# Rows of u broadcast by DMA instead of by TensorE in the mLSTM attention of a two-layer decoder trunk

## The reference, cut to what matters

```python
b = jnp.cumsum(lf, axis=-1)
logD = b[..., :, None] - b[..., None, :] + li[..., None, :]
m_t = jnp.maximum(inter, jnp.max(logD, axis=-1))
w_intra = jnp.exp(logD - m_t[..., None])           # exp(u[t] + w[s]), u = b - m_t, w = li - b
s = jnp.einsum('bhtd,bhsd->bhts', qc, kc) * w_intra
num = w_inter[..., None] * einsum(qc, C) + einsum(s, vc)
h = num / max(|den|, exp(-m_t))
C_new = decay[..., None, None] * C + jnp.einsum('bhs,bhsd,bhse->bhde', ws, kc, vc)
```

## Time and profile before

| | |
|---|---|
| median of 3 runs | 1389.44 us (1386.63 to 1391.36) |
| the profiled execution, its own time | 1389.6 us |
| its span | 1387.8 us, mean granted clock 0.98 |
| PE / PE weight load busy | 1334.1 us (96%) / 1289.9 us (93%) |
| DVE / ACT / POOL busy | 660.6 / 442.6 / 367.7 us (48%, 32%, 26%) |
| stage of the heads | about 211 us to 308 us of the span |

### The profile page before, as it was taken

How to read it: one execution, slowest core, us unless ns; L and a number is a source line. 1 busy time by engine, 2 the same in 40 slices (tenths; PEclk the granted TensorE clock), 3 DMA queues, 4 the chain that set the end, 5 groups by cost and what they waited for, 6 DMA issues and landing times.

```text
span 1387.8 us, 25466 instructions
## 1 busy us (share of the span) xinstructions
PE 1334.1 (96%) x10119; PEld 1289.9 (93%) x10119; DVE 660.6 (48%) x846; ACT 442.6 (32%) x672; POOL 367.7 (26%) x368
## 2 busy tenths in 40 slices
PE   4999999999999999999999896999999999999998
PEld 3999996779999999999999886999999999999997
DVE  6662333665794573343344693343533433333443
ACT  4311133432342241241341235322521422422423
POOL 3000004433799990000018561122000000000032
PEclk9999998999999999999999997999999999999999
DMA  5233231113332232223224985222222232323231
GB/s 146 62 84 84 76 91 28 53 43 76 92 88 79 78 89 80 87 76 90 76 76 141 155 138 130 85 81 85 77 83 84 76 90 76 91 76 91 76 89 72
DMA packets 239139, 119.55 MB, mean 86 GB/s; under 512 B 35512, under 2 KB 235888, under 8 KB 239088
## 3 DMA queue, kind: packets, MB, share of 16 engines
q1 hardware_dynamic: 238832, 118.78, 32.6%
q10 hardware_dynamic: 256, 0.06, 0.0%
HBM read 108.08 MB, written 10.73 MB: 86 GB/s over the span
## 4 chain that ended last, share of the span: by engine, by line
PE 85%; SPq 5%; DVE 5%; issue 1%; ACT 1%; DMA 1%; POOL 0%; DVEq 0%; ACTq 0%; POOLq 0%
PE ps L310 76%; SPq L521 2%; PE ps L1550 2%; PE ps L1577 2%; SPq L548 1%; DVE wlo L294 1%; DMA d_y<-U 1%; PE ps L1540 1%; PE ps L1586 1%; PE ps L1580 1%; DVE R L331 1%; PE ps L1603 1%; PE ps L1791 1%; SPq L502 0%; DVE xg_lo L360 0%
## 5 line engine op out<-in xcount | busy, mean ns | idle before, releaser
L289 ACT ACTIVATE whi<-raw 128x1024 fp32r<-128x1024 f32 x177 | 187.0, 1057 | 503.3 <-PE ps L310 491.0
L310 PE MATMUL ps<-hid_hi,whi 128*128 128x288 f32 x1408 | 302.9, 296 | 11.5 <-DVE hid_lo L1413 8.9
L310 PE MATMUL ps<-xg_hi,whi 128*128 128x288 f32 x1424 | 306.8, 297 | 3.0 <-DVE wlo L294 1.5
L310 PE MATMUL ps<-xg_lo,whi 128*128 128x288 f32 x1424 | 305.4, 295 | 0.0
L310 PE MATMUL ps<-xg_hi,wlo 128*128 128x288 f32 x1424 | 303.7, 294 | 0.0
L310 PE MATMUL ps<-hid_lo,whi 128*128 128x288 f32 x1408 | 302.0, 295 | 0.0
L310 PE MATMUL ps<-hid_hi,wlo 128*128 128x288 f32 x1408 | 300.7, 295 | 0.0
L294 DVE TENSOR_TENSOR wlo<-raw,whi 128x1024 fp32r<-128x1024 f32 x177 | 251.1, 1418 | 93.1 <-ACT whi L289 92.9
L310 PEld LDWEIGHTS ps<-hid_hi,whi 128*128 128x128 f32 x1408 | 226.0, 189 | 12.9 <-DVE hid_lo L1413 9.4
L310 PEld LDWEIGHTS ps<-xg_hi,whi 128*128 128x128 f32 x1424 | 228.4, 189 | 5.2 <-issue 2.3
L310 PEld LDWEIGHTS ps<-xg_hi,wlo 128*128 128x128 f32 x1424 | 229.0, 189 | 0.0
(11 more groups left out here) (351 smaller groups left out, 1132.1 us busy)
## 6 DMA issues: line engine op xcount, KB each, us to landing
raw<-in_ffn_w_up SPq DMA_DIRECT2D x64, 512.0 KB, 4.0
raw<-in_ffn_w_down SPq DMA_DIRECT2D x64, 512.0 KB, 3.7
raw<-in_mlstm_w_in SPq DMA_DIRECT2D x25, 512.0 KB, 3.8
raw<-in_s_w_glu SPq DMA_DIRECT2D x16, 512.0 KB, 3.9
raw<-in_mlstm_w_out SPq DMA_DIRECT2D x8, 512.0 KB, 3.7
late<-d_taps SPq DMA_DIRECT2D x64, 64.0 KB, 2.8
d_u<-unat SPq DMA_DIRECT2D x8, 288.0 KB, 2.8
U<-d_u SPq DMA_DIRECT2D x16, 144.0 KB, 6.7
```

The lines of the kernel that those rows point to most:

```text
L289: nc.scalar.activation(whi[:, s], raw[:, s], ACT.Copy).then_inc(whi_done, 1)
L310: last = nc.tensor.matmul(ps[:, 2 * s + c, 0:HN], w[:, s, k, :], a[:, k, c * HN:(c + 1) * HN], start=(k == 0 and n == 0), stop=(k == KT - ...
```

## The change

1. `spread` and its matmuls go. The eight rows u are written once to a DRAM scratch `d_ub` (after `m_ready`), and `load_u_row(h)` reads row h back with a zero step over 128 partitions into `Ub[h % 2]`, which lies in `acc` and `sqb`. `exps(h)` waits for that DMA (`ub_in`) and reads `Ub` in place of PSUM.
2. Rows 0 and 1 are loaded before the slabs 25 and following. Row h+2 is loaded in SP's loop over heads, directly after `load_state(h + 2)`; it waits for `exp_done` of head h too.
3. `load_state(h+2)` waits for the two state stores of head h alone; the store of `CP` is issued after the loads.
4. `sums(h)` waits for `qblk_ready` and `ncol_ready` only ahead of L1580.

```diff
+    d_ub = nc.dram_tensor("d_ub", (H, L), F32, kind="Internal").ap()
...
+        Ub = (acc[:, 0:L], sqb[:, 0:L])
...
                     load_slab(sp, 4 + q, j, slab_in[:, :, bass.ds((3 + q) * P + j * (2 * P), P)])
+            sp.wait_ge(m_ready, 1)
+            sp.dma_start(d_ub, qkvo[0:8, 24, TS:N]).then_inc(ub_out, 16)
+
+            def load_u_row(h):
+                if h < 2:
+                    sp.wait_ge(ub_out, 16)
+                    sp.wait_ge(acc_done, ACC0[1])
+                else:
+                    sp.wait_ge(exp_done, h - 1)
+                sp.dma_start(Ub[h % 2], d_ub[h:h + 1, :].to_broadcast([P, L])).then_inc(ub_in[h % 2], 16)
+
             load_slab(sp, 24, 0, slab_in[:, :, 23 * P:24 * P])
+            load_u_row(0)
+            load_u_row(1)
             load_slab(sp, 25, 0, slab_out[:, :, 0:P])
...
-                    sp.wait_ge(c_out[s], 16 * 3 * (h // 2))
+                    sp.wait_ge(c_out[s], 16 * 3 * (h // 2) - 16)
...
                                  Cst[b2 * DK:(b2 + 1) * DK, s, :, 0:DV]).then_inc(c_out[s], 16)
-                sp.dma_start(p_C[0, 0, h], CP[:, s, :]).then_inc(c_out[s], 16)
                 if h + 2 < H:
                     load_state(h + 2)
+                    load_u_row(h + 2)
+                sp.dma_start(p_C[0, 0, h], CP[:, s, :]).then_inc(c_out[s], 16)
...
-                act.wait_ge(u_done, h + 1)
+                act.wait_ge(ub_in[h % 2], 16 * (h // 2 + 1))
...
-                    last = nc.scalar.activation(e[:, OFF[j]:OFF[j] + w], ps[:, 0, j * P:L], ACT.Exp, bias=TK[:, 1 + j, h:h + 1])
+                    last = nc.scalar.activation(e[:, OFF[j]:OFF[j] + w], Ub[h % 2][:, j * P:L], ACT.Exp, bias=TK[:, 1 + j, h:h + 1])
...
-            def spread(h):
-
-                if h:
-                    pe.wait_ge(exp_done, h)
-                nc.tensor.matmul(ps[:, 0, :], SEL[:, h, :], qkvo[0:8, 24, TS:N], start=True, stop=True).then_inc(u_done, 1)
-
...
                 pe.wait_ge(p_masked, h + 1)
-                pe.wait_ge(qblk_ready, h + 1)
-                pe.wait_ge(ncol_ready, h + 1)
...
                 nc.tensor.matmul(ps[0:TS, 5, E1:2 * E1], e[0:TS, 1280:1344], Vtok[0:TS, 0, h, :], start=True, stop=True)
+                pe.wait_ge(qblk_ready, h + 1)
+                pe.wait_ge(ncol_ready, h + 1)
...
-            spread(0)
             scores(0)
-            spread(1)
...
-                if h + 2 < H:
-                    spread(h + 2)
```

More of the change, by code:

```diff
@@ L233, in build @@
             "att_const kv_done kv_act kv_dve osig_act osig_ready us_done us_arg us_exp es_ready")
-        (u_done, s_done, exp_done, p_done, p_masked) = sems(
-            "u_done s_done exp_done p_done p_masked")
+        (ub_out, s_done, exp_done, p_done, p_masked) = sems(
+            "ub_out s_done exp_done p_done p_masked")
         (qblk_ready, ncol_ready, pv_done, ot_act, ot_ready, ssq_done, ms_ready, rstd_ready, htok_ready,
@@ L259, in build @@
             "fin_pe fin_act fin_ready xf_ready yt_done y_act y_dve y_out out_done")
-        raw_in, ps_free, c_in, c_out, u2_in, y2_out = (
+        ub_in, raw_in, ps_free, c_in, c_out, u2_in, y2_out = (
             [ctx.enter_context(nc.semaphore(f"{n}{s}")) for s in range(2)]
-            for n in ("raw_in", "ps_free", "c_in", "c_out", "u2_in", "y2_out"))
+            for n in ("ub_in", "raw_in", "ps_free", "c_in", "c_out", "u2_in", "y2_out"))
         mt_in, yn_in = ([ctx.enter_context(nc.semaphore(f"{n}{k}")) for k in range(KT)] for n in ("mt_in", "yn_in"))
```

## The result

The changed kernel takes **1446.04 us** (median of 4 runs, 1444.55 to 1448.77) against 1390.4 us before (median of 4): ratio 1.0414, 95% interval 1.0392 to 1.0436 (the two medians divide to 1.040). The forecast was 1446 us, 1415 to 1458, slower at 0.96. The profiled execution took 1445.67 us, its span is 1443.0 us, 55.2 more than before.

A forecast was written before the change was run, and what follows sets the result against it. The prediction took PE, busy 96% of the span, to bound the kernel before. Five periods +52.5, start -1.8 and tail +5.8 gave +56.5 us on 1389.6, so 1446 us, range 1415 to 1458.

The forecast's parts named there:

- The spreads: On PE in the heads: removing six spreads of 1.05 us wins 0.79 us a head if nothing else held PE.
- The start: Ahead of the pipeline: two spreads removed gain 1.8 us, bounded by 1.0 and 2.3.
- The place of the row in SP's order: SP's loop over heads: row k+2 issued behind c_new(k), stores, their landing and state loads, 4.7 us after L1239 starts.
- Landing: The row's 256 KB DMA in the heads: lands 3.0 us after issue, at +7.7, so exponentials wait until +7.8.
- Rival C: Row DMA in the heads: reads queue and take 6.7 us, 3.7 more in six heads, +22, 1468 us; chance 0.11.
- The pieces on PE at the low clock: PE behind each gap at 1.2 GHz: updates_b 2.9, scores 5.0, updates_a 1.7 us.
- The clock: Heads: PE idles from about +5 to +10.5, clock falls to 0.50 each time, period 21.1 instead of 16.4 us.
- The tail: From c_new(5) to sums(7): 5.8 us later at the low clock.
- the five periods: Heads k = 0..4: period 21.1 instead of 10.6 us, together 52.5 us more.
- Parts 3 and 4: Store of CP and waits in sums: nothing, except head 7's 3.05 us stall goes, with exps(7) late in the same gap.
- B: Heads: same loop through SP at full clock, period 16.4 us, +29, 1419 us; chance 0.23 with its mixtures.
- D: ACT at L884: row there in time if landed 3.8 us before c_new(k), loop stays PE's, -11, 1378 us; chance 0.04.

The follow-up runs named there:

- e1: Changed kernel, with SP issuing the row of u for head h+2 ahead of its wait for c_new; 1381.18 us, ratio 0.9956 to the kernel before.
- e5: Changed kernel, with the row of u issued ahead of the c_new wait and the old waits of load_state and sums restored; 1380.6 us, ratio 0.9950.
- e6: Changed kernel plus eight extra unused matmuls in PE's gap behind heads_out of heads 0 to 5; 1426.22 us, ratio 1.0272.
- e2: Kernel before with only the two changes of waits (load_state and sums), the spreads staying on TensorE; 1385.37 us, ratio 0.9983.
- p3: Kernel before with only load_state waiting for the two state stores alone and CP stored behind the loads; 1385.3 us, ratio 0.9980.
- p4: Kernel before with only sums waiting for query block and normaliser column just ahead of the state matmuls; 1385.27 us, ratio 0.9980.
- e3: Changed kernel, with the row of u issued directly behind the wait for c_new, ahead of stores and state loads; 1406.54 us, ratio 1.013.
- e4: Changed kernel plus six extra unused matmuls in PE's gap behind heads_out of heads 0 to 5; 1435.6 us, ratio 1.0348.

## Why the prediction was right, point by point

- **The spreads.** 0.79 us a head was forecast for the case that nothing else holds PE; e1 and e5 show 0.78. The start was put at 1.8, between 1.0 and 2.3; it gave 1.1. The second scores waited 1.90 us for the first weights, which the estimate had named and priced too low: a term too large by 0.7 us.
- **The place of the row in SP's order.** Forecast: issued 4.7 us after the start of L1239 (L1255 after the change); measured 238.72 less 233.93, 4.8. This is shown as the cause by e1, where the place is the only thing that changed.
- **Landing.** The forecast was 3.0 us; measured were 3.3 to 3.5 for the six rows of the loop (up to 4.2 for one loaded ahead of the slabs). With the issue 0.1 later, the exponentials start 8.3 us after L1255 for 7.8: mis-sized by about 0.45 us a head. Rival C (6.7) did not come. The DMA issues by tensor after the change (count, KB each, median us to landing) answer to the earlier trace rows:

```profile
acc<-d_ub SPq DMA_DIRECT2D x4, 256.0 KB, 3.4
sqb<-d_ub SPq DMA_DIRECT2D x4, 256.0 KB, 3.5
...
out<-CP SPq DMA_DIRECT2D x8, 32.0 KB, 2.9
```

  The fit of the Trainium skill, "DMA: Bandwidth & Descriptors", in the section on the anatomy of a DMA, given for GpSimd's path, gave an estimated 2.6 us for this transfer. The measurement is 0.8 to 0.9 above it, and the measurement decides.
- **The exponentials** took 1.92 us from SBUF instead of 1.75 from PSUM, 0.17 a head not foreseen.
- **The pieces on PE at the low clock** were put at 2.9, 5.0 and 1.7; they took 2.64 (244.95 to 247.59), 4.96 and 1.59. This is 0.4 too much, and it cancels most of the two terms above. The period of 21.1 for 21.1 is thus luck in part, better than its parts deserve.
- **The clock.** Forecast as 0.50 after every gap; so it was in all six, with 4.63 us for each of the five score groups behind them. It is the idle gap that brings it about and not the 64 rows of the scores: the same scores run in 2.42 us in the kernel before, without a gap, and in four heads of e6, where useless work stands in it. The sentence that scores do not bring the clock back stands: after each gap they ran at the low level to their end, and it came back in the sums or behind them (0.50 from 256 to 258, 1.00 from 260 on). Whether their 64 rows are the reason was not tested. The Trainium skill, "TensorE: Matmul & The Clock Gate", section "HAM oscillation", describes a kernel that waits for a DMA in every turn and restarts at the low clock; the trace agrees, at about 3.8 us a head.
- **The tail and the sum.** The tail was put at 5.8 and took 5.85, the five periods at 52.5 and took 52.8. With the start of -1.1 the change's own parts make 57.5 us; the 1.9 us that this execution gained before the heads bring that back to the 55.6 measured up to `sums(7)`, next to the forecast of 56.5. That the median of 1446.04 meets the forecast so closely is luck in its last 2 us; the mechanism and its size are not.
- **Parts 3 and 4.** Nothing in the steady heads, and the stall at head 7 hidden behind `exps(7)`: both as forecast. By themselves they are worth 0.2% (e2, p3, p4).
- **The rivals.** B's full clock did not come in any of the six heads. D's case, a row that is there in time, is what e1 makes: 1381, where 1378 was given for it. D's condition was too strict: the row need not be there 3.8 us before `c_new(k)`, since about 2 us of waiting on ACT left the period of e1 at 9.79.

## What to carry to other kernels

Before a transfer is moved to a queue that issues in order, mark on the timeline when its data is wanted and when the instruction ahead of it in that queue is released; here the row was wanted 3.8 us before that release, and each head closed a loop over it. Place it by the moment its buffer is free (`exp_done`), not by the nearest similar load. And price a wait of TensorE twice, once as time and once as the matmuls behind it at half clock.

## What the runs showed of the hardware that I had not expected

- Useless matmuls paid: 43 us of them (6 times 7.13) made the kernel 20 us faster, 1426.2 for 1446.0.
- The clock has no simple answer to a short idle stretch. It held after 2.59 us in one head of e3 and fell after 3.11 in the next; it fell after 1.83 us in e4; in e6 it held after 1.53 and fell after 1.31. After a slab stall of 2.55 us it held in the kernel before, p3 and p4 and fell in e1, e2 and e5 (1.3 to 1.5 us). The first product, whose code the change does not touch, took 9.17 us in one execution and 8.03 in the other. Differences of 1 or 2 us in the span can come from such shifts and not from the edit.
- Four exponentials of 512 to 128 columns took 0.17 us more when their input lay in SBUF than in PSUM.
